# Placing the operands of the rounded-format matmuls at equal remainders modulo 512 bytes

## What is computed

```
x = layer_norm(ALPHA * x + even_mixer(x))       # one 1024x4096 projection; 4 heads of a gated
                                                # recurrence both ways, 8 heads of dilated attention;
                                                # one 1024x1024 projection
x = layer_norm(ALPHA * x + (silu(x @ w1) * (x @ w3)) @ w2)      # 1024 -> 2816 -> 1024
x = layer_norm(ALPHA * x + odd_mixer(x))        # 1024x3072; 8 heads of differential attention; 1024x1024
y = 0
for e in range(8):                              # top 2 of 8 experts for each token
    h = silu(x @ w1[e]) * (x @ w3[e])           # 1024 -> 2816
    y = y + gate[:, e] * (h @ w2[e])            # 2816 -> 1024
x = layer_norm(ALPHA * x + y)
```

## Time and profile before

| what | value |
|---|---|
| median of 3 executions | 1366.92 us (1364.84 to 1367.47) |
| the profiled execution | 1361.89 us, of which the span from first to last instruction 1360.1 us |
| TensorE busy | 95% of the span, 7164 matmuls |
| VectorE, ScalarE busy | 78%, 61% |
| mean granted TensorE clock | 0.973 of full speed |
| moved by DMA | 374.75 MB, 276 GB/s over the span |

### The profile page before, as it was taken

How to read it: one execution, slowest core, us unless ns; L and a number is a source line. 1 busy time by engine, 2 the same in 40 slices (tenths; PEclk the granted TensorE clock), 3 DMA queues, 4 the chain that set the end, 5 groups by cost and what they waited for, 6 DMA issues and landing times.

```text
span 1360.1 us, 20142 instructions
## 1 busy us (share of the span) xinstructions
PE 1288.9 (95%) x7164; PEld 1175.2 (86%) x7164; DVE 1062.2 (78%) x1007; ACT 835.5 (61%) x870; POOL 122.3 (9%) x108
## 2 busy tenths in 40 slices
PE   6998899999899987799999999999999999999996
PEld 5887778999787866699899899998998998998984
DVE  4777756544556995789889889889888898898997
ACT  3555352444433464277777777777777777787773
POOL 1035011000001831200000000000000000000000
PEclk8998969999999998799999999999999999999998
DMA  9652027766436541789999999999999999999990
GB/s 344 193 185 92 1 93 258 240 181 189 154 117 192 169 147 48 273 310 371 352 398 358 365 398 343 381 394 344 387 390 340 394 378 350 395 347 364 399 354 33
DMA packets 231280, 374.75 MB, mean 276 GB/s; under 512 B 8784, under 2 KB 156368, under 8 KB 231104
## 3 DMA queue, kind: packets, MB, share of 16 engines
q1 hardware_dynamic: 225344, 351.50, 73.7%
q0 software_dynamic: 5888, 22.61, 4.4%
HBM read 363.07 MB, written 11.01 MB: 275 GB/s over the span
## 4 chain that ended last, share of the span: by engine, by line
PE 85%; DVE 10%; issue 2%; ACT 1%; DMA 1%; POOL 0%; SPq 0%; DVEq 0%; ACTq 0%
PE psum L329 24%; PE psum L331 24%; PE psum L330 24%; DVE wlo L310 5%; PE psum L1754 1%; DMA raw<-in_ev_w_in 1%; PE psum L1386 1%; PE psum L1385 1%; PE psum L1384 1%; PE psum L1558 1%; PE psum L1542 1%; PE psum L1494 1%; PE psum L1407 1%; PE psum L1534 1%; PE psum L1409 1%
## 5 line engine op out<-in xcount | busy, mean ns | idle before, releaser
L310 DVE TENSOR_TENSOR wlo<-raw,whi 128x1408 fp32r<-128x1408 f32 (+2 forms) x493 | 785.6, 1612 | 202.0 <-ACT whi L303 198.4
L303 ACT CAST whi<-raw 128x1408 fp32r<-128x1408 f32 (+2 forms) x493 | 653.2, 1331 | 297.0 <-PE psum L331 273.1
L329 PE MATMUL psum<-whi,xe_hi 128*128 128x352 f32 x1024 | 332.8, 325 | 1.6 <-DVE mv L1329 1.6
L331 PE MATMUL psum<-whi,xe_lo 128*128 128x352 f32 x1024 | 330.9, 323 | 0.0
L330 PE MATMUL psum<-wlo,xe_hi 128*128 128x352 f32 x1024 | 330.6, 323 | 0.0
L329 PEld LDWEIGHTS psum<-whi,xe_hi 128*128 128x128 f32 x1024 | 192.5, 188 | 2.1 <-issue 1.8
L330 PEld LDWEIGHTS psum<-wlo,xe_hi 128*128 128x128 f32 x1024 | 192.4, 188 | 0.3
L331 PEld LDWEIGHTS psum<-whi,xe_lo 128*128 128x128 f32 x1024 | 192.6, 188 | 0.0
L329 PE MATMUL psum<-whi,xT_hi 128*128 128x512 f32 (+1 forms) x464 | 167.9, 362 | 9.6 <-DVE wlo L310 6.4
L330 PE MATMUL psum<-wlo,xT_hi 128*128 128x512 f32 (+1 forms) x464 | 166.8, 360 | 0.0
L331 PE MATMUL psum<-whi,xT_lo 128*128 128x512 f32 (+1 forms) x464 | 166.6, 359 | 0.0
(11 more groups left out here) (286 smaller groups left out, 1259.9 us busy)
## 6 DMA issues: line engine op xcount, KB each, us to landing
raw<-in_od_w SPq DMA_DIRECT2D x256, 704.0 KB, 6.9
raw<-in_od_w SPq DMA_DIRECT2D x94, 768.0 KB, 6.3
raw<-in_ev_w SPq DMA_DIRECT2D x32, 704.0 KB, 4.3
raw<-in_ev_w_in SPq DMA_DIRECT2D x32, 512.0 KB, 5.0
raw<-in_od_w SPq DMA_DIRECT2D x30, 512.0 KB, 6.2
raw<-in_od_w_in SPq DMA_DIRECT2D x24, 512.0 KB, 4.4
raw<-in_ev_w SPq DMA_DIRECT2D x12, 768.0 KB, 4.4
raw<-in_ev_w_out SPq DMA_DIRECT2D x8, 512.0 KB, 4.4
```

What stands on the lines that cost most here:

```text
L303: nc.scalar.copy(into[j][:, 0:kc * n], src[:, 0:kc * n]).then_inc(hi_done, 1)
L310: nc.vector.tensor_tensor(into[j][:, 0:kc * n], src[:, 0:kc * n], high[j][:, 0:kc * n].bitcast(F32), ALU.subtract).then_inc(lo_done, 1)
L329: nc.tensor.matmul(ps, hi[:, k, t0:t0 + P], w_h, start=(k == first_k), stop=False)
L331: last = nc.tensor.matmul(ps, lo[:, k, t0:t0 + P], w_h, start=False, stop=(k == last_k))
```

## The change

`phase`, where the overlaid tiles begin, is rounded up to the next address whose distance from the base is a multiple of 512 bytes, and so is `a0`. Everything placed by `phase` moves along with it. No instruction is added or taken away.

```diff
+        def in_phase(offset):
+
+            return base + (offset - base + 511) // 512 * 512
+
...
         vec = own("vec", [P, 96])
-        phase = cur[0]
+        phase = in_phase(cur[0])
...
-        a0 = oA - 20480
+        a0 = in_phase(oA - 20480)
         ah0 = [at(f"ah0_{j}", [P, 1024], F32R, a0 + 4096 * j)[0] for j in range(GT)]
         al0 = [at(f"al0_{j}", [P, 1024], F32R, a0 + 4096 * (GT + j))[0] for j in range(GT)]
```

## The result

| | before | changed |
|---|---|---|
| median | 1365.66 us (8 runs, 1362.38 to 1367.47) | 1358.39 us (8 runs, 1354.43 to 1360.16) |
| ratio of the times, 95% interval | | 0.9943 (0.9928 to 0.9958) |
| profiled execution, span | 1361.89, 1360.1 us | 1358.66, 1356.8 us |
| mean granted clock of that execution | 0.973 | 0.967 |

The change made the kernel 0.57% faster, 7.8 us of 1366 (5.7 to 9.8 by the interval). The forecast was a saving of 10.0 us and 1356.9 us, with a range of 1352.5 to 1362.5.

A forecast was written before the change was run, and what follows sets the result against it. TensorE, which never pauses in the routed part, was taken as the bound, through its matmul steps from start to start. Terms of 7.1+1.4+0.3+0.8+0.4 = 10.0 us off 1366.9 gave 1356.9 us, range 1352.5 to 1362.5.

The forecast's parts named there:

- Where the operands lie, and what a remainder costs: 512-column matmuls: four stretches of the old trace show 226.6 to 233.4 ns, set by both operands' remainders modulo 512 together.
- the rival without effect of addresses: All stages: addresses don't matter and the four rates have another cause; sum zero, 1366.9 us, chance 0.04.
- hTe: Routed experts' matmuls with hTe stationary: 1056 at 6.7 ns less each, saving 7.1 us.
- hT: Matmuls with hT stationary: 216 at 6.7 ns, saving 1.4 us, including 72 before a TensorE stop whose gain goes through.
- ah0: ah0 and al0 with xT, at the output projection: 48 matmuls at 6.8 ns, saving 0.3 us.
- xe: Routed experts' 352-column matmuls with xe: 3072 at 0.27 ns, saving 0.8 us.
- lev: lev with xT, 128 matmuls of 256 columns: half of 6.7 ns each, saving 0.4 us.
- Turns: Turns by the identity and plain float32 matmuls: taken at nothing; a nanosecond either way would be 0.2 us.
- The covers: Routed part: splits and transfers stay hidden behind TensorE, split slack 1.4 us shrinking by 0.2; otherwise 7.9 us would go.
- another bound: Rival, routed part: raw tiles or VectorE take over, 2.1 us of saving stay, 1364.8 us; chance 0.05.
- slower by the 352s: Rival, xe matmuls: level starts collide, 4.7 ns each over 3072 adds 14.4 us, giving 1372.1 us; chance 0.03.
- faster by the 352s: Rival, 352-column matmuls: they also come to 155.5 ns, another 14.1 us, giving 1343.6 us; chance 0.04.

The follow-up runs named there:

- the sweep: Seven edits of the changed kernel: everything behind `phase` at p bytes instead of 0, and ah0 at its own offset; 1358.90 to 1374.66 us.
- the common shift: Changed kernel with everything in SBUF moved on by 32 bytes together, all differences kept: 1357.81 us (9 runs), ratio 0.9951.
- p 448: Changed kernel with hTe and the others behind `phase` at 448 instead of 0, and ah0 at 64: 1363.92 us.
- p 288 and 416: Changed kernel with everything behind `phase` at 288 (ah0 at 96) or at 416 (ah0 at 224): 1372.90 and 1374.66 us.

## Why the prediction came out as it did

- *Where the operands lie, and what a remainder costs*: right. The four rates of before stood for the relation, the sweep and the common shift show it, and the rival without effect of addresses falls. The Trainium skill's SBUF — State Buffer, section Who interferes with whom, by which TensorE's two read ports are independent, doesn't foresee it: moving the stationary tile alone by 32 bytes changes its step by 6.5 ns. Two things of the reading were wrong. Not every inequality costs 6.7 ns: a difference of 64 costs 2.3, and of 256 nothing. And the 228.3 ns of ah1, from which the prediction took the low end of its range, is no step of a level pair but ten settling steps averaged with fourteen of 227.
- *hTe*, 7.1 us: 1056 x 6.4 = 6.8, shown by putting hTe alone off. From an expert's first hTe matmul to its last it is 0.81 us (30.17 instead of 30.98), 6.5 in eight.
- *hT*, 1.4 us: in the last group 233.3 became 226. Of its part before the stop of TensorE, 72 x 6.7 = 0.5 us, at least 0.3 came through: the changed execution was 4.68 us behind at the last ah0 matmul (223.59 against 218.91) and 4.36 at the first hT matmul behind the stop (377.60 against 373.24).
- *ah0*, 0.3 us: 48 x 6.8, as said. ah1, forecast unchanged at 228, came down to 226.7, since it needs no settling now; 0.1 us.
- *xe*, 0.8 us: 0.93 us an expert less hTe's 0.81 to 0.85 leaves some 0.1, 0.7 to 1.0 us in all. The size is right, and by luck: the 0.27 ns came from the first three blocks of an expert, which stayed at 160.1 and 160.0. The gain lies in the five blocks behind them, of which the prediction took no step: 161.7 to 162.1 ns before, 160.6 to 162.9 now, by starts.
- *lev*, 0.4 us: **the wrong sign**. 117.9 became 120.0, 0.3 us lost. The step of the prediction that failed is the scaling of a 512-column rate by columns, for lev and in "352 x 226.6/512 would be 155.8". lev moves at 64 over a stationary xT at 0, a difference of 64; at 512 columns that costs 2.3 ns, at 256 it saves 2.1. With p 448 (192 modulo 256) lev took 114.3 ns (14 steps, 124.41 to 126.01), 5.7 less than level, where the 512s pay 6.7 more: what is best depends on the width.
- *Turns*, nothing: h_e's turns take 109.1 ns instead of 108.5.
- *The covers*: held. No transfer and no split became the bound; VectorE, 88% busy before, has 84.84 us of 95 now. The down tile of rows 13 is ready at 754.17 + 1.76 = 755.93 us and begun at 757.21, 1.3 us later instead of 1.4: the slack shrank as said, and some remains.

The terms as measured make 7.5 (hTe and xe) + 1.4 + 0.4 - 0.3 = 9.0 us, against 10.0 forecast. The ratio gives 7.8 (5.7 to 9.8), the common shift 6.7 (4.4 to 9.0): the first interval holds 9.0, the second just reaches it. For the changed kernel the clock may make up most of what remains: its eight runs had 0.9683 in the mean, the 35 of before 0.9698 (not the eight of the comparison, whose clocks aren't known), and at 0.65 us a thousandth that is 1.0 us. For the common shift it doesn't: its nine runs had 0.9697, as the kernel before. hTe alone put off had 0.9677 in twelve. Whether placement nudges the clock, and where the last 1 to 2 us of the sum went, stays open.

The rivals: another bound fell with the waits; "no effect" with the sweep; "slower by the 352s" and "faster by the 352s" with xe at 160.0, in a single trace each, and with the time. But matmuls of 352 columns do collide at other places: at p 288 and 416 it costs 3.3 ns a matmul, more than the 3.0 from which the prediction saw the sign turn, and turns the gain into a loss.

## What to carry to other kernels

Where TensorE never pauses, measure the step from start to start, not the duration, leave out the first steps behind a change of tiles, and compare the same shape across the stages of one trace: a tuned kernel often holds the experiment already, here in four pairs of tiles. Where stationary tiles are placed by hand behind odd small tiles and the products are 512 columns wide, try a multiple of 256 bytes from the weights' tiles; it costs some hundred bytes and no instruction. And vary a placement before trusting it: two of the seven tried here made the kernel slower than where it began. Don't scale a cost of one width to another by the columns without a second width to check it on.

## What the runs showed of the hardware

- A rounded matmul of 128 x 128 with 512 moving columns takes 226.7 to 226.9 ns from start to start when both operands' addresses agree modulo 256, 229 at a difference of 64, and 232.3 to 234.3 at 32, 96, 128, 160, 192 and 224. What happens inside, TensorE's loading of the next weights beside the stream of columns colliding in SBUF, say, is argued and not shown; that LDWEIGHTS runs beside the matmuls is in the traces (89.59 us of 95 in the window in which the matmuls have 95.00).
- The width changes the order: at 256 columns a difference of 192 was the fastest (114.3 ns), then 64 (117.9), and level the slowest (120.0); at 352 level slices took 161.1, slices at 0 and 128 took 160.0 in one order and 161.1 in the other, and at 96 and 224 163.3.
- A step isn't set by addresses alone; what ran ahead counts. A level pair behind unequal ones needed some steps to settle (ten in the kernel before). The first three blocks of xe took 158.8 ns with hTe 32 bytes off and 160.0 with it level, at the same xe and whi. And one trace of the changed kernel has both: the second and third block of an expert took 15.10/95 = 158.9 ns in the first expert and 15.19/95 = 159.9 in the third, with the same tiles at the same addresses. What in the work ahead decides wasn't tried.

```profile
590.66 0.32 PE L333 MATMUL psum<-whi,xe_hi 128*128 128x352 f32 x1
...
605.76 0.32 PE L335 MATMUL psum<-whi,xe_lo 128*128 128x352 f32 x1
...
779.86 0.32 PE L333 MATMUL psum<-whi,xe_hi 128*128 128x352 f32 x1
...
795.05 0.33 PE L335 MATMUL psum<-whi,xe_lo 128*128 128x352 f32 x1
```

- Executions of one program differ by 5.7 us (the changed kernel, eight) and 7.6 us (the kernel before, 35), and the longer ones have the lower mean clock. In the two traces compared above the lower level lasted longer between 191 and 205 us (0.52 against 1.00); from 166 to 191 us both had 0.52.
